# Layer 0's query weights use idle halves of the key slots, its first output halves take two PSUM banks in turn, and layer 1 goes from projection to attention without a barrier

## What is computed

```python
for l in range(2):
    h, hc = pre_mod(x, ...), pre_mod(xc, ...)          # rms norm, scale, shift
    if l == 0: y, yc = mixer_ab(h, hc, ...)            # pooling mixer (512 channels) + windowed attention, 8 heads, 2 kv
    else:      y, yc = mixer_c(h, hc, ...)             # global attention, 16 heads, 4 kv, rms norm and rotary on q and k
    x = x + g1 * rms_norm(y)                           # and the context stream in layer 0
    x = x + g2 * rms_norm(conv_ffn(pre_mod(x, ...)))   # and the context stream in layer 0

def mixer_c(h, hc, w_qkv, w_out, ...):
    q, k, v = split_c(h @ w_qkv, q_g, k_g); qc, kc, vc = split_c(hc @ w_qkv, q_g, k_g)
    q, k = apply_rope(q, cos, sin), apply_rope(k, cos, sin)
    return softmax(q [k; kc]^T / 8) [v; vc] @ w_out
```

## Time and profile before

| | |
|---|---|
| timed runs, median (lowest, highest) | 1567.76 us (1566.34, 1568.14), three runs |
| profiled execution, time | 1565.17 us |
| profiled execution, span | 1563.4 us |
| mean granted TensorE clock | 0.982 |
| instructions | 22187 |

### The profile page before, as it was taken

One profiled execution on the slowest core, in us unless ns is written; L12 is line 12 of the kernel. 1 busy time (PEld: TensorE's weight loads), 2 busy tenths in 40 slices (PEclk: granted clock), 3 DMA queues, 4 the chain that ended last, 5 costly groups with the idle time before them and its releaser, 6 DMA issues.

```text
span 1563.4 us, 22187 instructions
## 1 busy us (share of the span) xinstructions
PE 1461.6 (93%) x7604; PEld 1194.5 (76%) x7604; DVE 969.8 (62%) x1484; ACT 715.4 (46%) x1230; POOL 585.0 (37%) x525
## 2 busy tenths in 40 slices
PE   3989889999999999999999698899999999999997
PEld 1877557778888888888888576678778888887886
DVE  3368787467678667834344657798876544445455
ACT  3323666444333233323353535487775544443453
POOL 2331554243222232313232522465543344443454
PEclk9999999999999999999999799999999999999999
DMA  8220850223455345411212113010003233332222
GB/s 353 53 94 5 294 181 9 82 95 93 131 168 166 116 131 153 143 39 61 69 61 69 55 34 108 28 41 1 1 1 95 82 94 94 95 103 78 94 94 101
DMA packets 129034, 147.06 MB, mean 94 GB/s; under 512 B 7284, under 2 KB 95608, under 8 KB 127936
## 3 DMA queue, kind: packets, MB, share of 16 engines
q1 hardware_dynamic: 128320, 145.81, 29.4%
q10 hardware_dynamic: 640, 0.26, 0.1%
HBM read 143.92 MB, written 2.14 MB: 93 GB/s over the span
## 4 chain that ended last, share of the span: by engine, by line
PE 84%; DVE 6%; ACT 4%; DMA 3%; issue 2%; POOL 2%; SPq 0%; ACTq 0%; DVEq 0%; POOLq 0%
PE ps L472 23%; PE ps L473 23%; PE ps L474 23%; PE ps L1470 4%; PE ps L1456 3%; PE ps L1481 2%; DMA start_w<-in_ada_w_dram 2%; PE ps L1483 2%; PE ps L1362 1%; ACT prob L1513 1%; PE ps L946 1%; DMA ada_w<-in_ada_w_dram 1%; PE ps L829 1%; DVE small L1585 0%; POOL prob L1645 0%
## 5 line engine op out<-in xcount | busy, mean ns | idle before, releaser
L464 POOL TENSOR_TENSOR w_lo<-raw,w_hi 128x1024 fp32r<-128x1024 f32 (+1 forms) x179 | 337.1, 1885 | 607.2 <-ACT w_hi L457 607.2
L472 PE MATMUL ps<-hT_hi,w_hi 128*128 128x512 f32 (+1 forms) x1096 | 387.6, 354 | 4.4 <-DVE hT_lo L1923 3.7
L473 PE MATMUL ps<-hT_lo,w_hi 128*128 128x512 f32 (+1 forms) x1096 | 385.3, 352 | 0.0
L474 PE MATMUL ps<-hT_hi,w_lo 128*128 128x512 f32 (+1 forms) x1096 | 382.9, 349 | 0.0
L457 ACT ACTIVATE w_hi<-raw 128x1024 fp32r<-128x1024 f32 (+1 forms) x200 | 173.2, 867 | 198.0 <-PE ps L474 166.1
L472 PEld LDWEIGHTS ps<-hT_hi,w_hi 128*128 128x128 f32 x1096 | 207.4, 189 | 41.4 <-DVE hT_lo L1923 5.6
L474 PEld LDWEIGHTS ps<-hT_hi,w_lo 128*128 128x128 f32 x1096 | 206.8, 189 | 28.9
L473 PEld LDWEIGHTS ps<-hT_lo,w_hi 128*128 128x128 f32 x1096 | 207.3, 189 | 26.7
L2353 DVE TENSOR_TENSOR g_lo<-act_g,g_hi 128x768 fp32r<-128x768 f32 (+1 forms) x82 | 103.9, 1273 | 149.3 <-ACT g_hi L2312 148.9
L472 PE MATMUL ps<-w_hi,g_hi 128*128 128x512 f32 x410 | 160.2, 391 | 5.0 <-DVE g_lo L2353 4.5
L474 PE MATMUL ps<-w_hi,g_lo 128*128 128x512 f32 x410 | 159.6, 389 | 0.0
(11 more groups left out here) (245 smaller groups left out, 2422.0 us busy)
## 6 DMA issues: line engine op xcount, KB each, us to landing
raw<-in_ffn_w_up_dram SPq DMA_DIRECT2D x84, 512.0 KB, 3.9
ada_w_up<-in_ada_w_dram SPq DMA_DIRECT2D x48, 512.0 KB, 4.1
raw<-in_ffn_w_down_dram SPq DMA_DIRECT2D x84, 256.0 KB, 2.6
ada_w<-in_ada_w_dram SPq DMA_DIRECT2D x32, 512.0 KB, 4.8
start_w<-in_ada_w_dram SPq DMA_DIRECT2D x8, 1024.0 KB, 8.5
raw<-in_c_w_qkv_dram SPq DMA_DIRECT2D x12, 512.0 KB, 3.7
raw<-in_ab_w_in_dram SPq DMA_DIRECT2D x8, 512.0 KB, 4.7
raw<-in_ab_w_out_dram SPq DMA_DIRECT2D x8, 512.0 KB, 4.5
```

Of the source, the lines that this page charges most:

```text
L464: by.tensor_tensor(w_lo[:, slot, 0:width], raw[:, n % RAW, 0:width], w_hi[:, slot, 0:width].bitcast(F32), ALU.subtract).then_inc(lo_split, 1)
L472: nc.tensor.matmul(outp, s_hi, m_hi, start=first, stop=False, skip_group_check=True)
L473: nc.tensor.matmul(outp, s_hi, m_lo, start=False, stop=False, skip_group_check=True)
L474: return nc.tensor.matmul(outp, s_lo, m_hi, start=False, stop=last, skip_group_check=True)
```

## The change

Layer 0: `query_half` places query chunk c in columns 512 to 1023 of key slot c (chunks 0 to 3, which the keys leave idle) and in columns 0 to 511 of the same slots (chunks 4 to 7). The splits of units 8 and 9 follow key tiles 1 and 2 on ACT (`QUERY_SPLITS`), unit 10 comes before and unit 11 after tile 5; DVE subtracts one behind each of the tiles 2 to 5. In attention the first halves alternate between bank 1 and bank 7, so that a W waits for the Y of two tiles before; the stage behind attention waits at its head for the third tile's square.

Layer 1: DVE's three splits stand ahead of the copies of tile nt - 3. The transposes of tile 9 come before tile 12, so that from then on they are two tiles late (`turned_behind`), those of the last tile within attention, as in layer 0. `close` and `after_phase` at this seam are gone, and DVE's attention waits for its own last projection step instead. The H steps come one fill slot later.

```diff
-    at = {3 * u + 1: [("H", u, 0)] for u in range(4)}
+    at = {3 * u + 2: [("H", u, 0)] for u in range(4)}
...
+        def query_half(c):
+            u, i = divmod(c, 2)
+            return 2 * (u % 2) + i, BANK * (u < 2)
...
+        def split_to(part, phase, m, width):
+            if halves(phase, m):
+                slot, c0 = query_half(2 * (m - 8))
+                return part[:, slot:slot + 2, c0:c0 + BANK]
+            return part[:, unit_slot(phase, m), 0:width]
...
             act.wait_ge(landed[n % RAW], turn * (16 * per_turn // RAW) + 16 * (n // RAW + 1))
-            if free:
+            if halves(phase, m):
+                act.wait_ge(used[phase], 2 * (m - 8) + 2)
+            elif free:
...
+        def turned_behind(l, n):
+            lag, late = TURN_LAG[l], l and n >= PROJ1_LATE
+            first = n - lag + int(late and n > PROJ1_LATE)
+            return range(max(first, 0), n - lag + 1 + int(late))
+
+        PROJ1_LATE = 11
...
-                            if n >= TURN_LAG[l]:
-                                turn(n - TURN_LAG[l])
+                            for old in turned_behind(l, n):
+                                turn(old)
...
-            if l:
-                for late in range(n - TURN_LAG[l], n):
-                    turn(late)
-                close(pe, "pe")
-            else:
-                turn(n - 2)
+            turn(n - 2)
             return lambda: turn(n - 1)
...
                         if l == 0 and gi < 2 and t == nt - 1:
-                            split_hi(act, phase, m, unit_width(l, m))
-                            m += 1
+                            split_hi(act, phase, 10, unit_width(l, 10))
...
-                        if l == 0 and gi < 2 and t == nt - 2:
-                            for i in range(2):
-                                split_hi(act, phase, m, unit_width(l, m))
-                                m += 1
-                        if l == 0 and gi < 2 and t == nt - 1:
-                            split_hi(act, phase, m, unit_width(l, m))
-                            m += 1
+                        if l == 0 and gi < 2 and t in QUERY_SPLITS:
+                            split_hi(act, phase, QUERY_SPLITS[t], unit_width(l, QUERY_SPLITS[t]))
...
+        QUERY_SPLITS = {1: 8, 2: 9, ALL_T - 1: 11}
...
                 if l:
                     nt = PROJ[l][gi][3]
-                    if gi < 2 and t == nt - 2:
-                        for m in range(4 * gi + 4, 4 * gi + 7):
-                            split_lo(dve, f"proj{l}", m, unit_width(l, m), by=nc.vector)
...
+                if l and gi < 2 and t == nt - 3:
+                    for m in range(4 * gi + 4, 4 * gi + 7):
+                        split_lo(dve, f"proj{l}", m, unit_width(l, m), by=nc.vector)
                 dve.wait_ge(steps, at)
                 buffers = 2
...
-                if l == 0 and kind == "kv" and t == PROJ[0][gi][3] - 2:
-                    for m in range(8, 11):
-                        split_lo(dve, "proj0", m, unit_width(0, m), by=nc.vector)
-                if l == 0 and kind == "kv" and t == PROJ[0][gi][3] - 1:
-                    split_lo(dve, "proj0", 11, unit_width(0, 11), by=nc.vector)
+                if l == 0 and kind == "kv" and t >= 2:
+                    split_lo(dve, "proj0", 6 + t, unit_width(0, 6 + t), by=nc.vector)
...
+        FIRST_HALF_BANKS = ((1, FILL_BANK), (FILL_BANK,))
...
-                            if k == 0 and g:
-                                pe.wait_ge(s(f"mixpost{l}_ysq"), g)
+                            if k == 0 and g >= len(FIRST_HALF_BANKS[l]):
+                                pe.wait_ge(s(f"mixpost{l}_ysq"), g - len(FIRST_HALF_BANKS[l]) + 1)
...
-                    elif l == 0 and h == 0:
-                        pe.wait_ge(s("turned_read0"), rope_plan(0)[1][ALL_T + 1])
-                    elif l == 0:
+                    elif h == 0:
+                        pe.wait_ge(s(f"turned_read{l}"), rope_plan(l)[1][ALL_T + 1])
+                    else:
                         last_turn()
...
-            if l:
-                after_phase(dve, before)
-            else:
-                dve.wait_ge(s("qk_steps0"), rope_plan(0)[0][-1])
+            dve.wait_ge(s(f"qk_steps{l}"), rope_plan(l)[0][-1])
...
+            if l == 0:
+                pe.wait_ge(s(f"{tag}_ysq"), OUT_DONE[0] - 1)
```

More of the change, by code:

```diff
@@ L449, in out_half0, with halves, split_from @@
                        k == 0, k == KC - 1)
+        def query_half(c):
+            u, i = divmod(c, 2)
+            return 2 * (u % 2) + i, BANK * (u < 2)
+        def halves(phase, m):
+            return phase == "proj0" and m >= 8
+        def split_to(part, phase, m, width):
[3 more added lines that the diff above has]
+            return part[:, unit_slot(phase, m), 0:width]
+        def split_from(phase, m, width):
+            v = raw[:, (FIRST_UNIT[phase] + m) % RAW, 0:width]
+            return v.rearrange("p (a n) -> p a n", a=2) if halves(phase, m) else v
         def split_hi(act, phase, m, width, turn=0, per_turn=0, free=True):
@@ L952, in wv @@
                 def wv(part, k, c0, w):
+                    if l == 0 and kind == "q":
+                        slot, at = query_half(k)
+                        return part[:, slot, at + c0:at + c0 + w]
                     slot = unit_slot(phase, m + k // 2)
@@ L1096, in proj_scalar @@
                             pool_hi(act, 0)
-                        if n >= TURN_LAG[l]:
-                            read_turned(n - TURN_LAG[l])
+                        for old in turned_behind(l, n):
+                            read_turned(old)
                         if l and gi < 2 and t == nt - 2:
@@ L1117, in proj_scalar @@
                     m += 1
-            for late in range(n - TURN_LAG[l], n):
+            for late in range(turned_behind(l, n - 1)[-1] + 1, n):
                 if l == 0 and late == n - 1:
@@ L1337, in hybrid_backbone_kernel, with first_half_acc @@
         O_BANK, FILL_BANK = 6, 7
+        FIRST_HALF_BANKS = ((1, FILL_BANK), (FILL_BANK,))
+        def first_half_acc(l, n):
+            return bank(FIRST_HALF_BANKS[l][n % len(FIRST_HALF_BANKS[l])])
         ADA0_ROW, ADA0_ROWS = 32, 8
@@ L1404, in ada0_columns, with attn_tensor @@
                                         ALU.mult).then_inc(s("gates_made0"), 1)
-        def attn_tensor(pe, l, before, last_turn=None):
+        def attn_tensor(pe, l, last_turn):
             groups, steps, first = attn_setup(l)
@@ L1411, in attn_tensor @@
             per = 2 if l == 0 else 1
-            if l:
-                after_phase(pe, before)
             per_tile = len([g for g in groups if g[1] == 0])
@@ L1486, in attn_tensor, with attn_scalar @@
             close(pe, "pe")
-        def attn_scalar(act, l, before):
+        def attn_scalar(act, l):
             groups, steps, first = attn_setup(l)
-            if l:
-                after_phase(act, before)
             for kind, g, i in steps:
@@ L1502, in attn_scalar @@
                         act.wait_ge(s(f"mixpost{l}_acc"), g + 1)
-                        first_half_scalar(act, f"mixpost{l}", four(bank(FILL_BANK)), y0_tile(l, g))
+                        acc = first_half_acc(l, g)
+                        first_half_scalar(act, f"mixpost{l}", four(acc), y0_tile(l, g))
                         act.wait_ge(s(f"mixpost{l}_y0"), g + 1)
-                        nc.scalar.activation(bank(FILL_BANK), bank(FILL_BANK), ACT.Square,
+                        nc.scalar.activation(acc, acc, ACT.Square,
                                              accum_out=ssum[:, 0, g:g + 1]).then_inc(s(f"mixpost{l}_ysq"), 1)
@@ L1545, in outputs_first, with attn_vector @@
             return out
-        def attn_vector(dve, l, before):
+        def attn_vector(dve, l):
             groups, steps, first = attn_setup(l)
             steps = outputs_first(steps)
-            if l:
-                after_phase(dve, before)
-            else:
-                dve.wait_ge(s("qk_steps0"), rope_plan(0)[0][-1])
+            dve.wait_ge(s(f"qk_steps{l}"), rope_plan(l)[0][-1])
             nden = 2 if l == 0 else 1
@@ L1628, in split_output, with attn_pool @@
                               ALU.subtract).then_inc(s(f"o_split{l}"), 1)
-        def attn_pool(pool, l, before):
+        def attn_pool(pool, l):
             groups, steps, first = attn_setup(l)
-            if l:
-                after_phase(pool, before)
             per = 2 if l == 0 else 1
@@ L2414, in _ @@
                 late = proj_tensor(pe, l)
-                attn_tensor(pe, l, b + 4, late)
+                attn_tensor(pe, l, late)
                 out_tensor(pe, l, NT[l])
@@ L2443, in _ @@
                 proj_pool(pool, l, b + 3)
-                attn_pool(pool, l, b + 4)
+                attn_pool(pool, l)
                 out_pool(pool, l, NT[l])
```

19 lines of the change are left out of this document (7 added, 12 removed).

## The result

| | kernel before | changed kernel |
|---|---|---|
| timed, median (lowest, highest) | 1567.63 us (1566.34, 1568.14), four runs | 1555.86 us (1552.54, 1556.43), four runs |
| ratio, 95% interval | | 0.9916 [0.9905, 0.9928] |
| once more, beside E9, E10 and E12 | 1568.35 us, nine runs | 1556.84 us, five runs; 0.9929 [0.9916, 0.9943] |
| profiled execution, time and span | 1565.17, 1563.4 us | 1552.54, 1550.8 us |
| mean granted TensorE clock of it | 0.982 | 0.987 |

The change makes the kernel some 12 us faster: 11.8 by the medians, 13.2 by the first ratio, 11.1 by the second. The forecast was 1557.3, within 1553.0 to 1561.5.

What follows compares the result with a forecast made beforehand. TensorE, busy 93% of the span, was taken as the bound, so only its waits could pay. Gains of 1.5 + 3.5 + 3.3 + 0 + 2.2 = 10.5 us gave 1557.3 us beside the median, range 1553.0 to 1561.5.

Steps and rivals of the forecast that it cites:

- (a): Layer 0's first query tile: query weights in idle halves let the fourth weight unit start 1.5 us earlier; bounds 0 to 2.
- feared fall among POOL's sums: Within (a): split 9 might fall among GpSimd's window sums and wait for one, half of 3.10 us.
- (b): Layer 0's attention: two banks in turn lift the 3.01 us wait for a square; transposes 3.5 us earlier, bounds 2.2 to 3.7.
- (c): Layer 1's key to query seam: splits ahead of the copies gain 3.3 us; bounds 2.8 to 3.7.
- second place: Same edit as (c), between layer 1's query groups: no gain, the 2.06 us wait for ScalarE's key copies stays; 0 to 1.6.
- (d): Layer 1's seam to attention: without barrier and transpose tail the first exponential comes 2.2 us sooner; 1.8 or 3.5 in other cases.
- signs of being wrong: Unit 11's split ends later, (b)'s idle moves to the out stage, or attention's first group takes back (d)'s gain.
- the table load follows at once: Within (d): ScalarE's 1.28 us load directly follows its last read, not the output cast; first exponential at 1004.15 for 1006.39.
- Part of it is not there: Rival, 25%: (a) gives 0, (b) 2.2, (d) 1.5; 7.0 us in all, or 1560.8.
- More than that: Rival, 13%: half-clock stretch between query groups goes too (1.6) and (d) gives 3.5; 13.5 us in all, 1554.3.
- It doesn't do what it says: Rival, 4%: an unseen wait takes each place's gain; within 3 us of before, 1565 to 1567.
- Slower: Rival, 3%: without the rests TensorE's clock falls in dense stages behind the seams; 1571.

Runs made afterwards that it cites:

- E9: E8 with one tiny exponential ahead of ScalarE's last read in layer 1's projection, to draw the table load forward; 1549.67 us, ratio 0.9891.
- E10: Changed kernel without part (c), layer 1's splits behind the copies again; 1559.06 us, ratio 0.9945 against the kernel before.
- E12: E9 with 18 unread transposes of the identity in TensorE's wait at layer 1's seam to attention; 1549.82 us, ratio 0.9888.
- E1: Kernel before with part (a) alone, query weights in idle key-slot halves and splits spread over tiles 2 to 5; 1565.53 us, ratio 0.9982.
- E5: Kernel before with first halves alternating between banks 1 and 7, each product still waiting for the square just before; 1567.38 us, ratio 0.9996.
- E3: Kernel before with part (c) alone, layer 1's three splits ahead of the copies; 1563.06 us, ratio 0.9963.
- E8: Changed kernel with layer 1's last key tile transposed behind tile 7 instead of tile 8; 1551.45 us, ratio 0.9903 against the kernel before.
- E6: Kernel before with only the output weights' casts one fill slot later, barrier and transposes kept; 1569.76 us, ratio 1.0005.
- E11: Changed kernel once more, unedited, for a second trace; 1556.84 us, ratio 0.9929 against the kernel before.

## Why the prediction was right, by its steps

- **(a)** 1.5 forecast, 1.5 over the traces. In E1, with key tile 2's last subtraction at 92.37 (92.28 before), split 10 starts at 104.11 (forecast: about 104.1), split 11 ends at 108.05 (108.1), and PE enters the tile at 101.75 (101.8). The feared fall among POOL's sums didn't happen: the row of 1.62 us is still there, and split 9 comes just behind it.
- **(b)** 3.5 forecast, 3.55 between the two first profiles, 3.0 over the traces. What is late next was named rightly: POOL's normalization, idle 0.85 for 0.9. The term mis-sized is the old form, not the new one. I took the lower clock behind the wait as a fixed part of it; three of seven traces don't have it, and there (b) gives 6.31 - 4.05 = 2.3, near the lower bound of 2.2. In all seven traces that turn the banks and lift the wait the distance is 4.03 to 4.05, without a lower clock, and E5, which turns them and keeps the wait, has the 6.30 of one bank. The Trainium skill, TensorE: Matmul & The Clock Gate, section "A second HAM failure mode: psum-queue depth-cycling", tells of a bf16 kernel in which PE's small idle pieces between groups made the clock go up and down; that would have kept a lower clock in the new form, and it is not borne out here.
- **(c)** 3.3 forecast, 3.3 over the traces. In E3's trace everything is 0.13 us later at the transposes; carried over to it, unit 7 was due at 942.0 and came at 942.03. At the second place nothing was forecast, and nothing came: the wait for ACT's copies stayed, and E8 shows that it was what the lower clock there hung on.
- **(d)** 2.2 forecast at the first exponential, 2.35 over the traces there (25.31 to 22.96), and 2.3 at the 21st. That it is so near is partly luck. By my sum the first exponential comes 1004.15 - 981.55 = 22.60 us after tile 8's transposes; it comes after 22.96, since the last transposes gain 0.4 us and not 0.7. Against the profile that I worked from (24.84) this is 1.9 us. The old form of the other traces is slower than that profile, because its lower-clock stretch at this seam was short (3.4 us for some 14). Between the two first profiles one of my signs of being wrong even showed: of 2.0 us at the first exponential 0.6 are left at the 21st (69.18 to 68.61). Only the five traces of each form take that back.
- **(d), what ended last.** The step "the table load follows at once" is right only together with the rest of (d), as E6 shows. In the kernel before, two things ended within 0.3 us of one another: the load (1004.85 + 1.28 = 1006.13) and head 0's maximum, for which the exponential waited last, until 1006.39. The cast ahead of the load was therefore not what held it back. Without the barrier the scores and the maximum come early, ScalarE's own chain is what is late, and only then does the cast count. I hadn't seen that the load's place before or behind the wait for the maximum depends on what stands ahead of it. My price for the moved casts, nothing, agrees with the whole change, in which the gain at the 21st exponential is that at the first; no run has it by itself.
- **The sum.** 10.1 us by places for 10.5, and 11 to 13 by timing. The traces show where one to three us more or less can come from. Between the two first profiles the places give 1.6 + 3.55 + 3.3 + 0.6 = 9.0 of the 12.6 us; nearly all of the rest lies where nothing was changed, 1.3 us ahead of key tile 2, 1.3 between (a) and (b), 0.85 between (b) and (c). E11's profile against the same profile of before gives 9.5 at the places and only 6.4 in all: it loses 1.6 us just ahead of (c) and 2.8 behind attention's 21st exponential, with stretches at the lower clock at 902 to 905 and 1165 to 1171 that the first two profiles don't have. So a single pair of profiles can miss the sum of the places by 3 us either way; how much of it is left in the medians stays open. The runs of E10's and E11's group have a mean clock of 0.978 in the kernel before and 0.982 in the changed one, which is 35.0 against 28.3 us of lost clock; how much of that reaches the end wasn't settled, since some of it lies beside waits, as at (c).
- **The rivals.** *Part of it is not there* is out as a whole: each part shows alone in its distance, though (b) gives only its 2.3 us where the lower clock does not come. *More than that* is out in its mechanism (the stretch between the query groups stayed), though the first profiled execution came near its 1554.3. *It doesn't do what it says* and *Slower* are out.

The Trainium skill, ScalarE: Activation LUTs, section "What ACT_TABLE_LOAD costs", gives a load as about 1283 ns and a drain of about 1380 ns with it. The rows here show the first and no trace of the second: in the changed kernel the read before the load ends at 991.04, the load begins at 991.06 and the exponential at 992.35, and taking the load away gave 1.4 us, not 2.7.

## What to carry to other kernels

Cost a seam by distances between rows that stand on both sides of it, not by clock times from the span's start, and where a stretch at the lower TensorE clock lies in it, cost it once with and once without. Look for the wait that ends last, and then for what is next: in all four places the next late thing could be read off before the change, to within some 0.5 us. And when PE waits for an accumulator's reader that sits behind a batch, ask whether the reading could be had one tile sooner: E8 got 3.9 us from two lines.

## What the runs showed of the hardware that I had not expected

- The lower clock does not follow an idle PE every time. Behind the 3.01 us wait of place (b) it came in four traces of seven, behind the 2.06 us wait between the query groups in 11 of 11. At the old seam to attention it lasted 3.4 us in one trace and some 14 in four others.
- Eighteen useless transposes in a wait of 2 us kept the clock (in one trace) at 1.00 over the next 10.6 us, in which PE was busy for 7.28 us only.
- Which side of a wait ScalarE's table load falls on can change with an unrelated instruction ahead of it, and with it 1.28 us.
